# Second block of a two-block transformer: the norms' factors moved from the inputs of the projections to their outputs

## The reference

```python
def rms_norm(x, g):
    return x * rsqrt(mean(x * x, -1) + eps) * g

for l in range(DEPTH):                              # DEPTH = 2
    h = rms_norm(x, attn_pre_norm[l])
    mix = hybrid_mixer(h, cos, sin, w_in[l], ...)   # h @ w_in, then three kinds of attention, then @ w_out
    x = x + rms_norm(mix, attn_post_norm[l])
    h = rms_norm(x, ffn_pre_norm[l])
    x = x + rms_norm(conv_ffn(h, w_up[l], conv_w[l], conv_b[l], w_down[l]), ffn_post_norm[l])

def conv_ffn(h, w_up, conv_w, conv_b, w_down):
    u = h @ w_up                                    # 1024 -> 2 * 2816
    c = conv_b + 3 causal taps of conv_w over u     # along the tokens
    a, b = split(c, 2)
    return (silu(a) * b) @ w_down
```

## Time and profile before

| what | value |
|---|---|
| median of 3 runs (lowest, highest) | 3058.23 us (3055.98, 3060.76) |
| the profiled execution | 3062.33 us, of which span 3060.5 us |
| granted clock of PE, mean over the span | 0.957 |
| PE busy | 93% of the span |
| DVE, ACT, POOL busy | 42%, 43%, 45% |
| read from memory | 355.5 MB, 117 GB/s |

### The profile page before, as it was taken

How to read it: one execution, slowest core, us unless ns; L and a number is a source line. 1 busy time by engine, 2 the same in 40 slices (tenths; PEclk the granted TensorE clock), 3 DMA queues, 4 the chain that set the end, 5 groups by cost and what they waited for, 6 DMA issues and landing times.

```text
span 3060.5 us, 44754 instructions
## 1 busy us (share of the span) xinstructions
PE 2840.4 (93%) x18684; PEld 2436.4 (80%) x18684; DVE 1300.1 (42%) x2725; ACT 1323.7 (43%) x2220; POOL 1380.3 (45%) x646
## 2 busy tenths in 40 slices
PE   6999998899998999998999899899898899899898
PEld 4778876688875888877788699899886799777897
DVE  2777767532234111015677653232236441173440
ACT  3254433323424322225454346444455564444563
POOL 3432030244432543435423177578652587532685
PEclk8999999999998999998999999899899999898899
DMA  6332022133324343334311154356443255431354
GB/s 227 117 110 80 28 76 80 45 119 95 117 84 161 117 145 125 115 124 162 97 49 49 35 166 147 116 160 180 145 134 106 92 184 172 123 131 53 128 182 122
DMA packets 103552, 359.45 MB, mean 117 GB/s; under 512 B 11126, under 2 KB 17526, under 8 KB 102840
## 3 DMA queue, kind: packets, MB, share of 16 engines
q1 hardware_dynamic: 103352, 356.60, 36.5%
HBM read 355.51 MB, written 1.05 MB: 117 GB/s over the span
## 4 chain that ended last, share of the span: by engine, by line
PE 82%; DVE 9%; ACT 6%; POOL 1%; issue 1%; DMA 1%; SPq 0%; DVEq 0%; ACTq 0%
PE PS L357 81%; DVE AR L1760 2%; DVE PS L1768 1%; ACT AR L1128 1%; POOL RINGL L2477 1%; ACT WH L1108 1%; PE PS L360 1%; ACT XT L1128 1%; DVE XT L1760 1%; DVE AR L1768 1%; DVE SM L1994 1%; ACT L1128 1%; DVE HT L1760 1%; DVE AR L1764 0%; DVE AR L1921 0%
## 5 line engine op out<-in xcount | busy, mean ns | idle before, releaser
L2477 POOL TENSOR_TENSOR RINGL<-RING,WH 128x1024 fp32r<-128x1024 f32 (+1 forms) x554 | 1299.2, 2356 | 1563.7 <-ACT WH L1108 1563.0
L357 PE MATMUL PS<-HTR,WH 128*128 128x256 f32 (+2 forms) x2736 | 885.0, 324 | 0.0
L1108 ACT ACTIVATE WH<-RING 128x1024 fp32r<-128x1024 f32 (+1 forms) x554 | 568.1, 1034 | 668.9 <-PE PS L357 538.4
L357 PE MATMUL PS<-HTH,WH 128*128 128x256 f32 (+1 forms) x2336 | 755.5, 324 | 33.7 <-POOL RINGL L2477 23.7
L357 PE MATMUL PS<-HTH,RINGL 128*128 128x256 f32 (+1 forms) x2336 | 726.5, 317 | 0.2 <-POOL RINGL L2477 0.2
L357 PE MATMUL PS<-ARR,WH 128*128 128x256 f32 (+2 forms) x2688 | 696.2, 327 | 26.6 <-POOL HTR L2482 9.9
L357 PEld LDWEIGHTS PS<-HTR,WH 128*128 128x128 f32 (+1 forms) x2736 | 531.3, 194 | 40.2 <-issue 1.6
L357 PEld LDWEIGHTS PS<-ARR,WH 128*128 128x128 f32 (+1 forms) x2688 | 471.3, 193 | 73.8 <-issue 16.4
L357 PEld LDWEIGHTS PS<-HTH,WH 128*128 128x128 f32 x2336 | 454.0, 194 | 75.4 <-issue 36.5
L357 PEld LDWEIGHTS PS<-HTH,RINGL 128*128 128x128 f32 x2336 | 444.5, 192 | 28.6 <-POOL RINGL L2477 0.4
L357 PE MATMUL PS<-ARR,RINGL 128*128 128x256 f32 (+1 forms) x1472 | 466.8, 327 | 0.0
(11 more groups left out here) (193 smaller groups left out, 3329.0 us busy)
## 6 DMA issues: line engine op xcount, KB each, us to landing
RING<-w_ada_in SPq DMA_DIRECT2D x96, 512.0 KB, 3.7
RING<-w_up_in SPq DMA_DIRECT2D x88, 512.0 KB, 3.2
RING<-w_gates_in SPq DMA_DIRECT2D x48, 512.0 KB, 3.6
RING<-w_ff_gate_in SPq DMA_DIRECT2D x44, 512.0 KB, 4.2
RING<-w_ff_up_in SPq DMA_DIRECT2D x44, 512.0 KB, 4.1
RING<-w_glu_in SPq DMA_DIRECT2D x32, 512.0 KB, 4.4
RING<-w_ff_down_in SPq DMA_DIRECT2D x32, 512.0 KB, 3.5
RING<-w_in_in SPq DMA_DIRECT2D x32, 512.0 KB, 3.6
```

What stands on the lines that cost most here:

```text
L357: return e.matmul(out_, lhsT, rhs, start=start, stop=stop)
L1108: e.activation(RINGS[name][:, j, 0:width], RING[:, b % NSLOT, 0:width], ACT.Copy).then_inc(*a_upper.up(b))
L2477: e.tensor_tensor(RINGL[:, i, 0:width], RING[:, i, 0:width], RINGS[name][:, j, 0:width], ALU.subtract).then_inc(*g_lower.up(b))
```

## The change

- The input of the projections is `XT` times the norm's weight alone (`ACT.Identity` with a column as scale writes the upper part `HN[0]`; `norm_lower` on DVE writes the lower part `HN[1]`), without the factor. `rms_lowers` on POOL is gone, and so are DVE's eight products into `HT`.
- ACT does upper part and square for each tile, right behind the residual's addition; `norm_lower` is put in DVE's program between the additions of `mix_out` (for the first norm: between the last multiplications of the first block's layer norm, whose affine part ACT does tile by tile just ahead).
- PE sums the squares between the products (`after=`): in `group` behind each k, in `w_t1` behind each block. The factor is spread (`normed_out`) after the group, or after the first block of `w_t0`.
- The factor is copied to SBUF (`RR` by tokens along the free axis, `RCOL` by tokens on the partitions) and multiplied into the outputs: into `v` and the gates through scales of instructions that are there already; into the tables of `rotate2` once (`ROPER`); into the five tiles that are not rotated by a DVE multiplication in place of ACT's copy (`raw2`); and into each of the 44 `w_up` tiles by one DVE multiplication in place in PSUM (`scaled`), for which ACT's conv now waits.
- DVE's feed-forward loop is written in a new order: it goes tile by tile, `scaled` of a tile ahead of the taps of the tile before.

```diff
@@ tensor, scalar, vector, gpsimd: cut to the core
...
-                normed((l, 2), None)
-                h = lambda k: g_norm.to("nlo", l, 2, k)
+                h = lambda k: d_norm.to("nlo", l, 2, k)
...
-                group(l, halves[0:3], HN, h, X)
+                group(l, halves[0:3], HN, h, X, lambda k: normed((l, 2), k))
+                normed_out((l, 2))
...
+                def sums(q):
+                    normed((l, 1), 2 * q)
+                    normed((l, 1), 2 * q + 1)
+
+                def factors(q):
+                    if q == 0:
+                        normed_out((l, 1))
+
+                project_tok("w_t1", l, 0, range(2), 284, 2, HN, h, lambda t: (d_mix, "t1", l, t), sums)
+                project_tok("w_t0", l, 0, range(2), 512, 2, HN, h, lambda t: (a_mix, "t0", l, t), factors)
...
+                    copy(HN[0](k, X), XT[:, k, X], ACT.Identity, scale=col(name, l, k)).then_inc(
+                        *a_norm.up("nhi", *nid, k))
                     copy(view({1: 14336, 2: 18432}[i], 8, 256)[:, k, :], XT[:, k, X], ACT.Square).then_inc(
                         *a_norm.up("rsq", *nid, k))
...
+            def norm_lower(nid, k):
+
+                l, i = nid
+                dve.wait_ge(*a_norm.to("nhi", *nid, k))
+                stt(HN[1](k, X), XT[:, k, X], col(("attn_pre_norm_2", "ffn_pre_norm_2")[i - 1], l, k), HN[0](k, X),
+                    ALU.mult, ALU.subtract).then_inc(*d_norm.up("nlo", *nid, k))
...
             def projections2(l):
                 product("w_t1", l, 0)
+                act.wait_ge(*d_norm.to("rr", l, 1))
...
             def ffn2(l):
                 def one(j):
-                    product("w_up", l, j)
+                    ahead("w_up", l, j)
+                    act.wait_ge(*d_ffn.to("scaled", l, j))
...
+                def scaled(j):
+                    b = ps("w_up", l, j)[:, 0:256]
+                    dve.wait_ge(*p_block.to("w_up", l, j))
+                    tt(b, b, RR, ALU.mult).then_inc(*d_ffn.up("scaled", l, j))
...
+                for n in range(2 * NFF + 1):
+                    if n < 2 * NFF:
+                        scaled(n % 2 * NFF + n // 2)
+                    if n:
+                        j = (n - 1) // 2
+                        two_taps((n - 1) % 2 * NFF + j)
+                        if n % 2 == 0:
+                            if j:
+                                lower(j - 1)
+                            dve.wait_ge(*a_ffn.to("silu", l, j))
+                            dve.wait_ge(*d_ffn.to("conv", l, j + NFF))
+                            tt(FFV[:, j, :], conv_tile(j), conv_tile(j + NFF), ALU.mult).then_inc(
+                                *d_ffn.up("ff2", l, j))
```

More of the change, by code:

```diff
@@ L401, in project, with group @@
                 stage_block[name, l, ct] = n
-            def group(l, items, src, ready, cols):
+            def group(l, items, src, ready, cols, after=lambda k: None):
                 hi, lo = src
@@ L1585, in normed @@
                              *a_norm.up("rsd", *nid))
[L1586 to L1591, removed]
             def projections2(l):
                 product("w_t1", l, 0)
+                act.wait_ge(*d_norm.to("rr", l, 1))
                 for t in range(2):
-                    copy(VX[:, t, 4:6, :], ps("w_t1", l, 0, t)[:, 0:256].rearrange("p (h n) -> p h n", h=2)).then_inc(
-                        *a_mix.up("v1", l, t))
+                    copy(VX[:, t, 4:6, :], ps("w_t1", l, 0, t)[:, 0:256].rearrange("p (h n) -> p h n", h=2),
+                         ACT.Identity, scale=RCOL[:, t:t + 1]).then_inc(*a_mix.up("v1", l, t))
                     act.wait_ge(*d_mix.to("t1", l, t))
@@ L1601, in projections2 @@
                 for t in range(2):
-                    copy(VX[:, t, 0:4, :], ps("w_t0", l, 0, t).rearrange("p (h n) -> p h n", h=4)).then_inc(
-                        *a_mix.up("t0", l, t))
+                    copy(VX[:, t, 0:4, :], ps("w_t0", l, 0, t).rearrange("p (h n) -> p h n", h=4),
+                         ACT.Identity, scale=RCOL[:, t:t + 1]).then_inc(*a_mix.up("t0", l, t))
                 act.wait_ge(*d_mix.to("t1", l, 1))
@@ L2260, in vector @@
                 residual(l, "w_ff_down")
-                layernorm(("p", l, 2), XT, XT, cols)
+                layernorm(("p", l, 2), XT, XT, cols, entry if last else lambda p, c, k: None)
+                if last:
+                    for k in range(5, 8):
+                        norm_lower((0, 1), k)
                 if not last:
@@ L2420, in mix_out @@
                 dve.wait_ge(*p_mix.to("frstd", l, name))
-                for k in range(9):
+                nid = (l, 2) if name == "w_mix" else (l + 1, 1)
+                for k in range(10):
                     if k < 8:
@@ L2438, in one, with lower @@
                         *d_ffn.up("conv", l, j))
-                for j in range(NFF + 1):
-                    if j < NFF:
-                        one(j)
-                        one(j + NFF)
-                    if j:
-                        dve.wait_ge(*a_ffn.to("hi2", l, j - 1))
-                        tt(FP2[1](j - 1, X), FFV[:, j - 1, :], FP2[0](j - 1, X), ALU.subtract).then_inc(
-                            *d_ffn.up("lo2", l, j - 1))
-                    if j < NFF:
-                        dve.wait_ge(*a_ffn.to("silu", l, j))
-                        dve.wait_ge(*d_ffn.to("conv", l, j + NFF))
-                        tt(FFV[:, j, :], conv_tile(j), conv_tile(j + NFF), ALU.mult).then_inc(*d_ffn.up("ff2", l, j))
+                def lower(j):
+                    dve.wait_ge(*a_ffn.to("hi2", l, j))
+                    tt(FP2[1](j, X), FFV[:, j, :], FP2[0](j, X), ALU.subtract).then_inc(*d_ffn.up("lo2", l, j))
+                for n in range(2 * NFF + 1):
[11 more added lines that the diff above has]
+                                *d_ffn.up("ff2", l, j))
+                lower(NFF - 1)
             dve.wait_ge(*cg_in.to(1))
             for l in range(DEPTH):
-                normed((l, 1), "attn_pre_norm_2")
+                normed((l, 1))
                 projections2(l)
@@ L2508, in gpsimd @@
                     norm_lower(("m", l, 2), 1, cols_of(l), k, *HB)
-            for l in range(DEPTH):
-                lowers(stage_block["w_t1", l, 0] + 1)
-                rms_lowers(l, 1)
-                lowers(stage_block["w_up", l, 0] + 1)
-                rms_lowers(l, 2)
             lowers(len(blocks))
```

119 lines of the change are left out of this document (66 added, 53 removed).

## The result

The changed kernel takes 3123.62 us (median of 4 runs, 3119.63 to 3124.33), where the kernel before took 3057.11 in the same rounds: 1.0214 times as long, interval 1.0200 to 1.0228. The forecast was 3107, within 3066 to 3130. The profiled execution has a span of 3122.4 us, 61.9 more than that of the kernel before; by the medians the change costs 66.5 (the profiled execution of the kernel before was 5.2 above its median in these rounds, this one 0.6).

A forecast was written before the change was run, and what follows sets the result against it. The prediction took PE, busy 93% of the span, to bound the kernel. Norms +4.3 and feed-forward loop +44.4 gave +48.7 on the profiled 3062.33, so 3111.0; less 4.1 for the median, 3107 us, range 3066 to 3130.

The forecast's parts named there:

- The feed-forward loop: Feed-forward parts: DVE's SBUF operations meet POOL's, weight blocks come late; six cycles in each layer, +44.4 us in both.
- A cycle: Feed-forward loop: three pairs, six tiles, cost 0.2 + 2.5 = 2.7 us in lateness, 3.7 with the clock's share.
- the clock was to be lost in two of three: Feed-forward loop: 1.6 us counted for two of three 2.5 us pauses, 1.0 a cycle.
- the 5 us pause ahead of them: Ahead of `w_up`'s fourth tile, layer 0: PE pauses 5 us and loses the clock, turning -2.9 into -1.9.
- The multiplication was put at 0.42: Feed-forward tiles: each `scaled` takes 0.42 us on DVE; 88 add 37 us, costing nothing alone.
- Rival A: Feed-forward loop not knocked out of step, only small lateness at each pair: 3070 to 3080 us, chance 0.22.
- The norms' places: The four norms: early starts largely lost again; -1.9, -3.1, +3.3, +5.2, and 0.8 for `raw2`, make +4.3 us.
- The starts: Behind the norms: products start 7 to 9 us earlier; the group after the first mixer 8.8 us earlier.
- its pauses ahead of `w_t0`'s blocks: Norms ahead of mixers: PE pauses 4.0 and 4.4 us, costing the clock about 1.0 to 1.3 each.
- the group needs 0.72 for a k: Mixer to feed-forward: group fed at 1.07 us a tile, upper-part products end about 2417.1, 6.7 us earlier.
- Rival B: Norms' early ends kept, -25.8 us, and the loop costing 7 to 12: 3032 to 3044 us, chance 0.12.

The follow-up runs named there:

- e1: Changed kernel with the 88 feed-forward multiplications replaced by one-column memsets, DVE's order and waits kept: 3109.4 us, 1.0178 of before.
- e2: Changed kernel with all multiplications, but DVE's feed-forward loop in the order of before: 3072.1 us, 1.0049 of before.
- e3: Changed kernel in its own order, but ff2 and `lower` read one of their two inputs from PSUM: 3085.91 us, 1.0091 of before.
- e4: Changed kernel, but ACT writes `w_up`'s upper parts up to three blocks ahead instead of two: 3071.95 us, 1.0049 of before.
- e10: e9 plus constant matmuls on PE around the spreading of the residual's factor, results unused: 3049.81 us, 0.9972 of before.
- e9: e5 plus `w_up`'s fourth to sixth upper parts behind the root and layer 1's feed-forward norm sums in PSUM bank 7: 3051.43 us, 0.9978 of before.
- e5: e4 plus `w_t0`'s upper parts early: first two blocks ahead of the root, other two ahead of the copies of v: 3056.89 us, 0.9991 of before.
- e7: e5 and e6 together, on top of e4: 3054.22 us, 0.9987 of before.
- e8: Kernel before the change with only the one-line edit of e4, ACT three blocks ahead in `w_up`: 3060.18 us, 0.9999 of before.
- e11: Kernel before the change with e10's constant matmuls in the residual, and 3 and 4 more around the spreading of the norm's factor: 3061.15 us, 1.0016.
- e6: e4 plus `w_up`'s fourth upper part ahead of the norm's tiles, fifth and sixth right behind the root: 3076.29 us, 1.0056 of before.
- e12: e10 with DVE's feed-forward loop in the order of before, as in e2: 3069.93 us, 1.0034 of before.

## Why the prediction was right, and what in it was mis-sized

**The feed-forward loop** was worked out as six late blocks in each layer, each from `lower` blocked, ff2 blocked behind it for 2.6 us, then a late `scaled` and a late upper part. The trace has it so: in layer 0 `lower` takes 1.67 to 1.68 and ff2 2.62 us seven times, at every third pair, and six late blocks follow between the fourth tile and `w_down` (the seventh delays `w_down` itself). DVE and PE in order of time:

```profile
2466.71 1.68 DVE L1779 TENSOR_TENSOR ARR<-AR,ARR 128x256 fp32r<-128x256 f32 x1
2468.31 2.62 DVE L1779 TENSOR_TENSOR AR<-AR 128x256 f32<-128x256 f32 x1
...
2558.96 0.36 PE L360 MATMUL PS<-HTH,WH 128*128 128x256 f32 x1 [2.22 <-POOL RINGL L2533]
```

A cycle was to cost 2.7 and costs 2.6 (19.92 less 17.34); the clock was to be lost in two of three and is lost in two of six, for 1.4 us. The length of the pause does not tell which, as two in a row show (the first matmul of 0.36 us is at full clock, the one of 0.55 is not):

```profile
2456.55 0.36 PE L360 MATMUL PS<-HTH,WH 128*128 128x256 f32 x1 [2.23 <-POOL RINGL L2533]
...
2476.47 0.55 PE L360 MATMUL PS<-HTH,WH 128*128 128x256 f32 x1 [2.22 <-POOL RINGL L2533]
```

From the fourth tile to `w_down` 120.2 us became 141.7: +21.4 in layer 0, +21.8 in layer 1, against 22.2 for each. That this is so close is in part luck. The five full cycles of layer 0 lost 15.7 us, 3.1 each, not 3.7; the first five tiles lost 4.5, of which 2.3 is the low clock behind the 5 us pause ahead of them, a term that the prediction had put, with 1.0, into the norms' part. The multiplication was put at 0.42 and is 0.429 by DVE's groups by form:

```profile
L1779 DVE TENSOR_TENSOR PS<-PS,RS 128x256 f32<-128x256 f32 x88 | 37.5, 429 | 98.3 <-PE PS L360 98.3
```

e1, e2, e3 and e4 each remove one link (work, order, two SBUF inputs, the late upper part), and only e1 leaves the stalls. Rival A was not the case; e2 and e4 come to its time, e2 without its lateness at each pair. Two of the prediction's sums do not come out as written: a cycle with the clock lost each time is 2.7 + 1.6 = 4.3, twelve times 51.6, not 53; and A's 3058 + 4 + 7 to 12 is 3069 to 3074, not up to 3080. Neither moves the forecast.

**The norms' places** are the mis-sized term. They were summed to +3.5 (-1.9, -3.1, +3.3, +5.2) and are +16.9: root to fourth tile +1.1 and +3.5, the mixers' +7.7 and +4.5. The starts came as worked out: PE begins the group 2.5 us behind DVE's first operation of the residual (3.0 were expected), and its pauses ahead of `w_t0`'s blocks are near what was expected (4.0 and 4.4):

```profile
2219.59 0.47 PE L360 MATMUL PS<-WH,HTH 128*128 128x512 f32 x1 [3.89 <-POOL RINGL L2533]
2232.43 0.80 PE L360 MATMUL PS<-WH,HTH 128*128 128x512 f32 x1 [4.15 <-POOL RINGL L2533]
```

What failed is the step by which "the group needs 0.72 for a k" and its products with upper parts end at 2417.1, that is 9.3 us behind its start: it took the full clock. They took 13.1 us (2415.44 to 2428.55), and what follows up to the fourth tile 9.0, just as worked out (2417.1 to 2426.1). The table by stretch of the changed kernel says 0.50 for five of the eight k:

```profile
2416.00:2424.00 8.00, 8.00 (x58) 6.42 (x58) 6.12 (x17) 4.81 (x12) 0.00 (x0) 0.50 0.01 2
2424.00:2426.00 2.00, 2.00 (x22) 1.55 (x20) 0.00 (x0) 0.00 (x0) 0.00 (x0) 0.77 0.00 0
```

58 matmuls took 8 us; in e10, at full clock, 90 go into 8 us. An earlier start bought slower matmuls: PE had been idle for 1.78 and 2.52 us around the spreading of the residual's factor, and it works at the 1.2 GHz level until some 9 us into the group. e10 shows that cause by removing it: root to fourth tile takes 19.8 us there and 22.3 in e9, in both layers. The 0.72 also leaves out the sums of squares that now stand behind each k: at full clock a k takes 1.16 in all, at half 1.95. At full clock that would have cost little, since DVE feeds a k every 1.12. Behind `w_t0`'s two pauses the clock cost more than the 1.0 to 1.3 put down for each: first block and spreading took 5.77 us for some 3.8 at full clock, the last two blocks 7.98 for 5.45. Two smaller things were missing altogether: the bank that layer 1's sums of squares wait for (3.17 us, e9), and `w_down`, 2.7 and 1.4 us longer. The clock is low there too, before and after at the start of `w_down` in layer 0 (behind pauses of 1.69 and 2.58 us):

```profile
2549.00:2551.00 2.00, 1.76 (x14) 1.76 (x15) 1.28 (x4) 1.11 (x3) 0.00 (x0) 1.00 0.45 161
```

```profile
2579.00:2581.00 2.00, 1.77 (x8) 1.77 (x9) 2.00 (x2) 0.00 (x0) 2.00 (x1) 0.50 0.10 40
```

In the profiled executions the forecast was +48.7 and the difference is 61.9: the norms' places 13.4 more, `w_down` 4.1 more, the loop 1.2 less, the rest (the mixers' rest, the first block and the end) 3.1 less.

**Rival B** (early ends kept) had its condition right: with the weight parts ready, e5, e7 and e9 keep them. Its price was too high: -25.8 for the four places was worked out, and e9 has -4.1 and -7.3 at the two mixers and -0.2 from the root to `w_down` in layer 0. The best kernels here, e9 and e10, are 0.2 to 0.3% faster than the kernel before; none reached the 3032 to 3044 that B forecast.

## What to carry to other kernels

Before an operation is added to an engine that is half idle, list which of its neighbours read two operands from SBUF, and where GpSimd works at that moment: in the order of before the 88 multiplications made the way from the fourth tile to `w_down` 2.8 and 0.5 us longer (e2), while the place into which the new order put two other operations cost 43 us with them and some 38 without (e1). Where a producer delivers just in time (0.7 us to spare), give it one more block of lead before anything else; here one line did as much as the reordering, and the two together did harm, so repairs of one stall are to be measured one at a time and together. An earlier start of TensorE is worth its matmuls at the clock that the trace grants at that place, not at full clock.

## What the hardware did that I had not expected

- The rest of mixer 0 took 159.2 us before, 160.5 in the changed kernel, 161.9 in e8 and 166.3 in e11, though e8 and e11 do not touch it. By stretches its tail has the same matmuls at another clock, before and then in e11:

```profile
2352.00:2387.00 35.00, 30.84 (x167) 22.18 (x164) 18.03 (x60) 13.27 (x40) 6.35 (x3) 0.95 0.09 31
```

```profile
2346.00:2387.00 41.00, 36.53 (x170) 25.34 (x168) 19.12 (x62) 13.90 (x43) 7.03 (x3) 0.81 0.08 29
```

  Six microseconds between two executions of the same instructions, from 0.95 to 0.81 of the clock in a stretch where PE often pauses briefly; it is as large as what e7 to e11 try to tell apart. The other profiled executions fall into two groups: 160.4 to 160.5 us in the changed kernel, e1, e2, e3, e4 and e6, and 161.9 to 162.2 in e5, e7, e8, e9, e10 and e12. Values that repeat so closely speak for shifts ahead of the stretch and against chance, but with one trace for each kernel that is not shown.
- The first block, which no kernel here changes, reached its last root between 2187.7 us (e5) and 2201.1 us (e9) of the profiled span. Stretches from a common event told more than whole spans.
- Here GpSimd was held up little where the two meet, DVE for a whole GpSimd instruction: in e4 DVE's two operations took 2.47 and 2.62 us in a row in place of 0.42, while GpSimd's weight parts in that feed-forward loop took 2.36 to 2.61, against 2.34 to 2.41 in e2, where nothing collides.
